# Five rotating lanes for the RG-LRU recurrence: the convolution of tile j+1 issued ahead of the decays of tile j

## The chip, the cores and the metric

One core of one Trainium2 chip runs the whole kernel. The metric is the device time of one execution in microseconds (us). PE is TensorE's matmul side, PEld its weight loads, DVE is VectorE, ACT is ScalarE, POOL is GpSimd, SP is the engine that issues most DMAs.

## The reference

One layer over 1024 tokens of width 1024, in float32. After an RMSNorm, one projection gives two 512-wide inputs of a recurrent branch and the queries, keys and values of a windowed attention. The recurrent branch is what the change touches:

```python
lx = causal_depthwise_conv(lx, w_conv[i], b_conv[i])      # 4 taps along the tokens
r  = sigmoid(blockdiag(lx, w_a) + b_a)
ig = sigmoid(blockdiag(lx, w_i) + b_i)
a  = exp(LRU_C * r * log_sigmoid(lam))
h_t = a_t * h_(t-1) + sqrt(1 - a_t**2) * (ig * lx)_t       # scan over 1024 tokens
y_lru = rmsnorm(h * gelu(lg), g_lru_out)
```

Both branches are normed, concatenated, projected and added to x. Then come a squared-ReLU MLP of width 4096, a gated per-layer embedding and a final RMSNorm.

## The kernel before

Everything lies transposed in SBUF: features on the 128 partitions, the 1024 tokens along the free axis, in two halves of 512. Every product runs as three matmuls (L451 to L453): each float32 operand is split into a high part (ACT copies) and a low part (DVE or POOL subtracts). Weights come in pieces of two halves: SP loads `stage`, ACT writes `w_hi` (`high`, L724), POOL writes `w_lo` (`low`, L353).

The input projection is 28 groups of 24 matmuls; group g goes to bank g % 4 and waits until DVE has emptied that bank from group g-4 (`evac`, L1036, which multiplies by the norm and signals main_free). Groups 0 to 7 give the four tiles (128 channels) of the recurrence's input, 8 to 15 the gelu inputs `gl`, 16 to 19 keys and values, 20 to 27 the queries. Into this stream the recurrence of the four tiles is woven. For tile j, with GATE_AT = [5, 9, 13, 17]:

- DVE: `conv(j)` (L1072) makes `lru_x` from `yl[:, j]` in one tensor_scalar and three scalar_tensor_tensor steps. `lru_x` is a single buffer, so from tile 1 on conv(j) waits for state_done of tile j-1.
- ACT: `gate_input_high(j)` (L790) copies `lru_x` to `gx_hi` in two halves. POOL: `gate_input_low(j)` (L382) writes `gx_lo` in two halves.
- PE: `gates(j)` (L502), 12 matmuls in the middle of group 6, 10, 14 or 18, six for each half, each six waiting for gx_low.
- ACT: `lru_gates(j)` (L796): four sigmoids, a tanh, an exponential. From tile 1 on they wait for state_done of tile j-1.
- DVE: `decays(j)` (L1089), ACT: the root (L823), DVE: `states(j)` (L1102), a multiplication and the scan along the tokens, from `lru_x` into `yl[:, j]`.

The queues are in program order. DVE's order is the loop at L1199:

```python
for g in range(4, IN_GROUPS - 2):
    if g + 1 in GATE_AT[1:]:
        conv(GATE_AT.index(g + 1))
    evac(g)
    if g - 1 in GATE_AT:
        decays(GATE_AT.index(g - 1))
    if g - 2 in GATE_AT:
        states(GATE_AT.index(g - 2))
```

conv(0) stands ahead of the loop (L1135). ACT's order is the loop at L811: at g = 8, 12, 16 it copies two halves of `w_hi`, at g = 5, 9, 13, 17 it makes gx_hi and the gate functions, at the g after that the root, and at 15 and 18 two Gelus. POOL's loop (L391) makes the two halves of `w_lo` and then `gx_lo` of one tile in each turn. Behind the projection follow `multiply_y`, squares and norm of the branch (`norm_y`, `low_y`), and the attention, whose values `v_win` (16 chunks of keys' values, turned on PE and copied by ACT at L840) lie at T + 8 KB, over `lru_u` and `lru_x`.

Of the kernel before, what the change touches and what calls it, by code (L numbers as in the profile page):

```python
# [9 lines left out]
ALU = mybir.AluOpType  # L10
ACT = mybir.ActivationFunctionType
AX = mybir.AxisListType

P = 128
SEQ = 1024
# [4 lines left out]
LT = LRU // P  # L20
# [68 lines left out]
def build(nc, x, p, vectors, gates_w, w_in, w_out, w_ff1, w_ff2, w_ple_gate, w_ple_proj, alibi, out):  # L89
    ctx = ExitStack()  # L90
    with ctx:
# [3 lines left out]
        def at(name, offset, shape, dt=F32):  # L95
            return nc.alloc_sbuf_tensor_at(name, shape, dt, offset=base + offset)
# [23 lines left out]
        lru_r = at("lru_r", T, [P, SEQ])  # L120
        lru_i = at("lru_i", T + 4 * KB, [P, SEQ])
        lru_u = at("lru_u", T + 8 * KB, [P, SEQ])
        lru_x = at("lru_x", T + 12 * KB, [P, SEQ])
        yl = at("yl", Y, [P, LT, SEQ])
        gl = at("gl", G, [P, LT, SEQ])
        r_lru = at("r_lru", G + 12 * KB, [P, SEQ])

        qT = at("qT", Q, [P, SEQ // CHUNK, LT, CHUNK])
        kT = at("kT", KV, [P, PAD + SEQ])
        vT = at("vT", KV + 4 * (PAD + SEQ), [P, PAD + SEQ])  # L130
        v_win = at("v_win", T + 8 * KB, [P, SEQ // CHUNK, P])
        prob = at("prob", G, [P, 2, 1024])
        probT = at("probT", G + 8 * KB, [P, 1024])
        bias = at("bias", G + 12 * KB, [P, 512])
# [71 lines left out]
        def half(hf):  # L206
            return slice(hf * HALF, (hf + 1) * HALF)
# [4 lines left out]

        def q_tile(j, hf):
            return qT[:, hf * 8:(hf + 1) * 8, j, :]

        def by_chunk(ap):
            return ap.rearrange("p (c q) -> p c q", q=CHUNK)
# [127 lines left out]
        def _(pool):  # L345
# [36 lines left out]
            def gate_input_low(j):  # L382

                if j >= 1:
                    pool.wait_ge(gates_done, 4 * j)
                for hf in range(2):
                    pool.wait_ge(gx_high, 2 * j + hf + 1)
                    pool.tensor_tensor(gx_lo[:, half(hf)], lru_x[:, half(hf)], gx_hi[:, half(hf)], ALU.subtract
                                       ).then_inc(gx_low, 1)

            for n in range(2, IN_PIECES):  # L391
# [56 lines left out]
        def _(pe):  # L448
# [110 lines left out]
            def values(u):  # L559

                pe.wait_ge(pt0_read, u + 1)
                pe.wait_ge(pt1_read, u + 1)
                if u >= 1:
                    pe.wait_ge(o_read, u)
                else:
                    pe.wait_ge(main_free, L0)
                for cp in range(2):
                    for g in range(NKV):
                        last = pe.matmul(bank[3][g * HD:(g + 1) * HD, cp * 256:(cp + 1) * 256],  # L569
                                         v_win[:, 2 * u + cp, g * HD:(g + 1) * HD],  # L570
                                         probT[:, g * 512 + cp * 256:g * 512 + (cp + 1) * 256],
                                         start=True, stop=True)
                last.then_inc(o_done, 1)
# [149 lines left out]
        def _(act):  # L723
# [66 lines left out]
            def gate_input_high(j):  # L790

                act.wait_ge(conv_done, j + 1)
                for hf in range(2):
                    act.activation(gx_hi[:, half(hf)], lru_x[:, half(hf)], ACT.Copy).then_inc(gx_high, 1)

            def lru_gates(j):  # L796

# [13 lines left out]
            for g in range(IN_GROUPS):  # L811
                if g % 4 == 0 and g >= 4:
                    n = g // 4 + 1
                    piece_free(act, n - 2)
                    high(2 * n)
                    high(2 * n + 1)
                if g in GATE_AT:
                    gate_input_high(GATE_AT.index(g))
                    lru_gates(GATE_AT.index(g))
                if g - 1 in GATE_AT:  # L820
                    j = GATE_AT.index(g - 1)
                    act.wait_ge(lru_m2, j + 1)
                    act.activation(lru_u[:, :], lru_u[:, :], ACT.Sqrt).then_inc(lru_root, 1)  # L823
                if g in (15, 18):
                    for j in (2 * (g == 18), 2 * (g == 18) + 1):
                        act.wait_ge(main_free, 12 if g == 15 else 16)
                        act.activation(gl[:, j, :], gl[:, j, :], ACT.Gelu_apprx_tanh).then_inc(gelu_done, 1)
                if g in (20, 21):
                    hf = g - 20
                    act.wait_ge(state_done, LT)  # L830
                    for j in range(LT):
                        act.wait_ge(y_done, j + 1)
                        square(SQ_BY[SS_LRU + hf] - 4 + j, sq, yl[:, j, half(hf)])
                if g in (22, 23):
                    root(SS_LRU + g - 22, 5, r_lru, LRU)
                if 21 <= g < 25:
                    i = g - 21
                    act.wait_ge(vt_done, i + 1)
                    act.wait_ge(state_done, LT)
                    act.activation(v_win[:, 4 * i:4 * i + 4, :], bank[6 + i % 2][:, :].rearrange(  # L840
                        "p (c d) -> p c d", d=P), ACT.Copy).then_inc(vt_read, 1)

            def exps(u):
                act.wait_ge(max_done, u + 1)
# [6 lines left out]
            def lru_high(hf):  # L851
                act.wait_ge(main_done, IN_GROUPS - 2 + 2 * hf)
                for j in range(LT):
                    act.wait_ge(y_normed, 4 * hf + j + 1)
                    split_high(H_LRU + 4 * hf + j, yl[:, j, half(hf)], None, j, hf)

            lru_high(0)
            exps(0)
# [152 lines left out]
        def _(dve):  # L1011
# [24 lines left out]
            def evac(g):  # L1036

                n, hf, m = g // 4, (g % 4) // 2, g % 2
                dve.wait_ge(main_done, g + 1)
                if n < 2:  # L1040
                    dst = yl[:, 2 * n + m, half(hf)]
                elif n < 4:
                    dst = gl[:, 2 * (n - 2) + m, half(hf)]
                elif n == 4:
                    dst = (kT, vT)[m][:, PAD + hf * HALF:PAD + (hf + 1) * HALF]
                else:
                    dst = q_tile(2 * (n - 5) + m, hf)
                src, r = main_bank(g)[0][:, :], r_mix[:, half(hf)]
                if n >= 5:
                    src, r = by_chunk(src), by_chunk(r)  # L1050
                dve.tensor_tensor(dst, src, r, ALU.mult).then_inc(main_free, 1)
# [20 lines left out]
            def conv(j):  # L1072

                dve.wait_ge(main_free, 4 if j < 2 else 8)
                if j >= 1:
                    dve.wait_ge(state_done, j)
                link(dve.tensor_scalar(lru_x[:, :], yl[:, j, :], v_conv[:, 12 + j:13 + j], v_bconv[:, j:j + 1],
                                       ALU.mult, ALU.add))
                for s in (1, 2, 3):
                    c = 4 * (3 - s) + j  # L1080
                    ins = dve.scalar_tensor_tensor(out=lru_x[:, s:], in0=yl[:, j, 0:SEQ - s],
                                                   scalar=v_conv[:, c:c + 1], in1=lru_x[:, s:],
                                                   op0=ALU.mult, op1=ALU.add)
                    if s < 3:
                        link(ins)
                    else:
                        ins.then_inc(conv_done, 1)

            def decays(j):  # L1089
# [7 lines left out]

                dve.tensor_scalar(lru_u[:, :], lru_u[:, :], 1e-34, None, ALU.max).then_inc(lru_m2, 1)
                dve.wait_ge(conv_done, j + 1)
                link(dve.tensor_tensor(lru_x[:, :], lru_i[:, :], lru_x[:, :], ALU.mult))  # L1100

            def states(j):  # L1102
                dve.wait_ge(lru_root, j + 1)
                link(dve.tensor_tensor(lru_x[:, :], lru_x[:, :], lru_u[:, :], ALU.mult))
                dve.tensor_tensor_scan(yl[:, j, :], lru_r[:, :], lru_x[:, :], 0.0, ALU.mult, ALU.add
                                       ).then_inc(state_done, 1)


            dve.memset(kT[:, 0:PAD], 0.0).then_inc(pads_ready, 1)
# [28 lines left out]
            def multiply_y(j):  # L1138
                dve.wait_ge(gelu_done, j + 1)
                dve.wait_ge(state_done, j + 1)  # L1140
                dve.tensor_tensor(yl[:, j, :], yl[:, j, :], gl[:, j, :], ALU.mult).then_inc(y_done, 1)

            def norm_y(hf):

                for j in range(LT):
                    dve.wait_ge(sq_done, SQ_BY[SS_LRU + hf] - 3 + j)
                    dve.scalar_tensor_tensor(out=yl[:, j, half(hf)], in0=yl[:, j, half(hf)],
                                             scalar=v_lru[:, j:j + 1], in1=r_lru[:, half(hf)],
                                             op0=ALU.mult, op1=ALU.mult).then_inc(y_normed, 1)

            def low_y(hf):
                for j in range(LT):
                    dve.wait_ge(y_normed, 4 * hf + j + 1)
                    split_low(H_LRU + 4 * hf + j, yl[:, j, half(hf)], None, j, hf)

            def softmax_front(u):

# [39 lines left out]
                dve.tensor_tensor(dst, main_bank(L0 + g)[0][:, :], dst, ALU.add).then_inc(main_free, 1)  # L1197

            for g in range(4, IN_GROUPS - 2):  # L1199
                if g + 1 in GATE_AT[1:]:  # L1200
                    conv(GATE_AT.index(g + 1))
                evac(g)
                if g - 1 in GATE_AT:
                    decays(GATE_AT.index(g - 1))
                if g - 2 in GATE_AT:
# [234 lines left out]
```

## Time and profile before

| what | value |
|---|---|
| runs of the kernel | 1176.6, 1175.78, 1176.55 us; median 1176.55 |
| profiled execution, first to last instruction (span) | 1174.1 us |
| median of the runs less that span | 2.45 us |
| mean granted TensorE clock | 0.985 |

For the profiled execution only the span is known; a run's time also has what lies around the first and last instruction, and it is set beside the median by the 2.45 us in the table. A row of a timeline has the start, the duration, the engine, the line and operation, out<-in, the shape and the count; in brackets stands how long the engine was idle before and what released it. Several like instructions in a row are merged (x2); a row's start is then that of the first.

### The profile page before, as it was taken

How to read it: one execution, taken by the hardware profiler on the slowest of the kernel's cores; microseconds unless marked ns; L12 is line 12 of the kernel's file. 1: busy time of each engine (PE TensorE's matmuls, PEld its weight loads, DVE VectorE, ACT ScalarE, POOL GpSimd, SP SyncE). 2: the span in 40 equal slices, each digit the busy share in tenths (PEclk: the TensorE clock that was granted, in tenths of full speed). 3: DMA queues.
4: the chain of work that ended last, by engine and by line, in shares of the span. 5: the costliest groups of instructions: out<-in, count | busy, mean ns of one | idle time of the engine just before them, and what ended most of it. 6: DMA issues, size and time to landing. Idle time of an engine off the chain costs nothing.

```text
span 1174.1 us, 13976 instructions
## 1 busy us (share of the span) xinstructions
PE 1120.6 (95%) x5196; PEld 922.6 (79%) x5196; DVE 692.3 (59%) x869; ACT 363.6 (31%) x597; POOL 394.9 (34%) x207
## 2 busy tenths in 40 slices
PE   7999899899989999999999999999999999989996
PEld 5777688677768888888888888888888888867995
DVE  6966848767996445445444444444444434586677
ACT  8544554345532211211111111111111111445445
POOL 2633252330481311311311212212213113376874
PEclk9999999899989999999999999999999999989998
DMA  7211102110221111111211201211211211122243
GB/s 269 73 36 36 36 1 81 37 37 1 72 72 36 52 56 36 55 52 36 63 44 36 71 36 36 71 36 36 71 36 41 66 36 53 54 72 72 99 153 109
DMA packets 22481, 69.43 MB, mean 59 GB/s; under 512 B 2352, under 2 KB 4400, under 8 KB 22448
## 3 DMA queue, kind: packets, MB, share of 16 engines
q1 hardware_dynamic: 22176, 67.95, 17.1%
q10 hardware_dynamic: 272, 1.05, 0.2%
q8 instruction: 20, 0.33, 0.1%
q14 instruction: 13, 0.11, 0.0%
HBM read 64.79 MB, written 4.19 MB: 59 GB/s over the span
## 4 chain that ended last, share of the span: by engine, by line
PE 84%; DVE 10%; issue 3%; ACT 1%; DMA 1%; SPq 0%; DVEq 0%
PE bank L451 27%; PE bank L452 27%; PE bank L453 27%; DVE h_lo L1029 4%; DVE xT L1257 1%; DVE r_mix L1034 1%; PE bank L541 1%; DVE scaled L1255 1%; PE bank L569 1%; DMA stage<-in_w_in 1%; PE bank L555 1%; DVE o_ring L1354 1%; PE bank L499 1%; DVE acc L272 0%; DVE xT L1305 0%
## 5 line engine op out<-in xcount | busy, mean ns | idle before, releaser
L451 PE MATMUL bank<-h_hi,w_hi 128*128 128x512 f32 (+1 forms) x1056 | 407.6, 386 | 25.3 <-DVE h_lo L1029 17.5
L452 PE MATMUL bank<-h_lo,w_hi 128*128 128x512 f32 (+1 forms) x1056 | 400.4, 379 | 0.0
L453 PE MATMUL bank<-h_hi,w_lo 128*128 128x512 f32 (+1 forms) x1056 | 400.3, 379 | 0.0
L421 POOL TENSOR_TENSOR w_lo<-stage,w_hi 128x1024 fp32r<-128x1024 f32 x64 | 152.6, 2405 | 524.4 <-ACT w_hi L927 524.4
L1305 DVE TENSOR_TENSOR xT<-bank,xT 128x512 f32<-128x512 f32 x256 | 176.2, 690 | 142.7 <-PE bank L453 142.4
L451 PEld LDWEIGHTS bank<-h_hi,w_hi 128*128 128x128 f32 x1056 | 200.7, 190 | 72.7 <-issue 10.2
L452 PEld LDWEIGHTS bank<-h_lo,w_hi 128*128 128x128 f32 x1056 | 200.8, 190 | 37.3 <-issue 1.7
L453 PEld LDWEIGHTS bank<-h_hi,w_lo 128*128 128x128 f32 x1056 | 200.3, 190 | 37.4
L451 PE MATMUL bank<-u_hi,w_hi 128*128 128x512 f32 x512 | 199.2, 389 | 0.0
L452 PE MATMUL bank<-u_lo,w_hi 128*128 128x512 f32 x512 | 199.2, 389 | 0.0
L453 PE MATMUL bank<-u_hi,w_lo 128*128 128x512 f32 x512 | 199.2, 389 | 0.0
L1290 DVE SCALAR_TENSOR_TENSOR relu<-bank,r_ffn 128x512 f32<-128x512 f32 x64 | 44.2, 691 | 213.4 <-PE bank L453 212.9
L927 ACT ACTIVATE w_hi<-stage 128x1024 fp32r<-128x1024 f32 x64 | 64.0, 1048 | 286.9 <-DVE xT L1305 286.9
L359 POOL TENSOR_TENSOR w_lo<-stage,w_hi 128x1024 fp32r<-128x1024 f32 x45 | 120.7, 2702 | 86.9 <-ACT w_hi L730 86.9
L938 ACT ACTIVATE u_hi<-relu 128x512 fp32r<-128x512 f32 x64 | 40.5, 633 | 279.4 <-DVE relu L1290 279.4
L451 PEld LDWEIGHTS bank<-u_hi,w_hi 128*128 128x128 f32 x512 | 96.1, 188 | 19.9
L452 PEld LDWEIGHTS bank<-u_lo,w_hi 128*128 128x128 f32 x512 | 96.1, 188 | 19.9
L453 PEld LDWEIGHTS bank<-u_hi,w_lo 128*128 128x128 f32 x512 | 96.1, 188 | 19.9
L272 POOL TENSOR_TENSOR acc<-acc,sq 128x512 f32<-128x512 f32 (+1 forms) x60 | 77.8, 1297 | 53.3 <-ACT sq L752 39.0
L1029 DVE SCALAR_TENSOR_TENSOR h_lo<-xT,vec,h_hi 128x512 fp32r<-128x512 f32 x48 | 62.6, 1325 | 3.7 <-ACT h_hi L744 3.5
L1294 DVE TENSOR_TENSOR usq<-relu 128x512 f32<-128x512 f32 x64 | 50.1, 783 | 2.2
L730 ACT ACTIVATE w_hi<-stage 128x1024 fp32r<-128x1024 f32 x45 | 44.9, 1046 | 6.1 <-PE bank L453 6.1
(141 smaller groups left out, 845.6 us busy)
## 6 DMA issues: line engine op xcount, KB each, us to landing
stage<-in_w_ff SPq DMA_DIRECT2D x64, 512.0 KB, 3.3
stage<-in_w_ple_gate SPq DMA_DIRECT2D x24, 512.0 KB, 3.3
stage<-in_w_in SPq DMA_DIRECT2D x13, 512.0 KB, 3.3
stage<-in_w_out SPq DMA_DIRECT2D x8, 512.0 KB, 3.5
xT<-in_x SPq DMA_DIRECT2D x7, 512.0 KB, 9.4
out_x<-o_ring SPq DMA_DIRECT2D x4, 512.0 KB, 4.0
out_x<-o_ring SPq DMA_DIRECT2D x7, 256.0 KB, 2.2
pT<-in_p ACTq DMA_DIRECT2D x1, 1024.0 KB, 7.7
```

The costliest lines, as they stand in the source:

```text
L272: eng.tensor_tensor(dst, dst, src, ALU.add).then_inc(sq_used, 1)
L359: pool.tensor_tensor(lo, stage[:, s % STAGES, :], hi, ALU.subtract).then_inc(w_split, 1)
L421: pool.tensor_tensor(w_lo[:, n0 % 2, o:o + HP], stage[:, s0 % STAGES, :], w_hi[:, n0 % 2, o:o + HP], ALU.subtract).then_inc(w_split, 1)
L451: pe.matmul(o, whi, hh, start=first, stop=False)
L452: pe.matmul(o, whi, hl, start=False, stop=False)
L453: return pe.matmul(o, wlo, hh, start=False, stop=last)
L730: act.activation(hi, stage[:, s % STAGES, :], ACT.Copy).then_inc(w_high, 1)
L927: act.activation(w_hi[:, n0 % 2, o:o + HP], stage[:, s0 % STAGES, :], ACT.Copy).then_inc(w_high, 1)
L1029: dve.scalar_tensor_tensor(out=o, in0=src, scalar=scale, in1=hi, op0=ALU.mult, op1=ALU.subtract).then_inc(h_ready, 1)
L1290: dve.scalar_tensor_tensor(out=relu[:, j % 2, :], in0=bank[j][:, :], scalar=0.0, in1=r_ffn[:, half(hf)], op0=ALU.max, op1=ALU.mult).then_i ...
L1294: dve.tensor_tensor(usq[:, j % 2, :], relu[:, j % 2, :], relu[:, j % 2, :], ALU.mult).then_inc(u_sq, 1)
L1305: dve.tensor_tensor(dst, bank[4 + q % 4][:, :], dst, ALU.add).then_inc(y_added, 1)
```

## The change

The single buffer `lru_x` and the four tiles of `yl` become one tile `lane` of five buffers. The projection's tile j is evacuated into lane j+1 (`lx(j)`). The convolution of tile j reads lane j+1 and writes lane j (`yl(j)`), which is free as soon as conv(j-1) has read it; the gate product, the multiplication by the root and the scan then work in place in lane j. conv(j+1) waits for conv_done of tile j instead of its state_done, and stands behind the evacuation of groups 4, 8 and 12, that is ahead of decays(j). Two waits are added: ACT waits for gates_done of tile j-1 before it overwrites `gx_hi` (POOL had that wait already), and DVE waits for gx_low before it multiplies lane j in place. As lane 0 now lies where the second half of `v_win` was, `v_win` becomes two tiles, `v_first` in its old place and `v_second` over lane 4.

```diff
-        lru_x = at("lru_x", T + 12 * KB, [P, SEQ])
-        yl = at("yl", Y, [P, LT, SEQ])
+        lane = at("lane", T + 12 * KB, [P, LT + 1, SEQ])
...
-        v_win = at("v_win", T + 8 * KB, [P, SEQ // CHUNK, P])
+        v_first = at("v_first", T + 8 * KB, [P, SEQ // CHUNK // 2, P])
+        v_second = at("v_second", Y + 12 * KB, [P, SEQ // CHUNK // 2, P])
...
+        def lx(j):
+            return lane[:, j + 1, :]
+
+        def yl(j):
+            return lane[:, j, :]
+
+        def v_win(c):
+            return (v_first, v_second)[c // 8], c % 8
...
-                    pool.tensor_tensor(gx_lo[:, half(hf)], lru_x[:, half(hf)], gx_hi[:, half(hf)], ALU.subtract
+                    pool.tensor_tensor(gx_lo[:, half(hf)], yl(j)[:, half(hf)], gx_hi[:, half(hf)], ALU.subtract
...
                 act.wait_ge(conv_done, j + 1)
+                if j >= 1:
+                    act.wait_ge(gates_done, 4 * j)
                 for hf in range(2):
-                    act.activation(gx_hi[:, half(hf)], lru_x[:, half(hf)], ACT.Copy).then_inc(gx_high, 1)
+                    act.activation(gx_hi[:, half(hf)], yl(j)[:, half(hf)], ACT.Copy).then_inc(gx_high, 1)
...
                 if n < 2:
-                    dst = yl[:, 2 * n + m, half(hf)]
+                    dst = lx(2 * n + m)[:, half(hf)]
...
                 if j >= 1:
-                    dve.wait_ge(state_done, j)
-                link(dve.tensor_scalar(lru_x[:, :], yl[:, j, :], v_conv[:, 12 + j:13 + j], v_bconv[:, j:j + 1],
-                                       ALU.mult, ALU.add))
+                    dve.wait_ge(conv_done, j)
+                o, x_j = yl(j), lx(j)
+                link(dve.tensor_scalar(o, x_j, v_conv[:, 12 + j:13 + j], v_bconv[:, j:j + 1], ALU.mult, ALU.add))
                 for s in (1, 2, 3):
                     c = 4 * (3 - s) + j
-                    ins = dve.scalar_tensor_tensor(out=lru_x[:, s:], in0=yl[:, j, 0:SEQ - s],
-                                                   scalar=v_conv[:, c:c + 1], in1=lru_x[:, s:],
-                                                   op0=ALU.mult, op1=ALU.add)
+                    ins = dve.scalar_tensor_tensor(out=o[:, s:], in0=x_j[:, 0:SEQ - s], scalar=v_conv[:, c:c + 1],
+                                                   in1=o[:, s:], op0=ALU.mult, op1=ALU.add)
...
                 dve.wait_ge(conv_done, j + 1)
-                link(dve.tensor_tensor(lru_x[:, :], lru_i[:, :], lru_x[:, :], ALU.mult))
+                dve.wait_ge(gx_low, 2 * j + 2)
+                link(dve.tensor_tensor(yl(j), lru_i[:, :], yl(j), ALU.mult))
...
-                link(dve.tensor_tensor(lru_x[:, :], lru_x[:, :], lru_u[:, :], ALU.mult))
-                dve.tensor_tensor_scan(yl[:, j, :], lru_r[:, :], lru_x[:, :], 0.0, ALU.mult, ALU.add
-                                       ).then_inc(state_done, 1)
+                link(dve.tensor_tensor(yl(j), yl(j), lru_u[:, :], ALU.mult))
+                dve.tensor_tensor_scan(yl(j), lru_r[:, :], yl(j), 0.0, ALU.mult, ALU.add).then_inc(state_done, 1)
...
             for g in range(4, IN_GROUPS - 2):
-                if g + 1 in GATE_AT[1:]:
-                    conv(GATE_AT.index(g + 1))
                 evac(g)
+                if g + 1 in GATE_AT:
+                    j = GATE_AT.index(g + 1) + 1
+                    if j < LT:
+                        conv(j)
                 if g - 1 in GATE_AT:
                     decays(GATE_AT.index(g - 1))
```

The other places that read `yl[:, j]` or `v_win` (squares, norm, splits, the value matmuls and their copies) read the same data under the new names.

## Rows read from the trace of the kernel before

**Rows 1.** The page's first part: busy us of each engine, share of the span, instructions.
```profile
PE 1120.6 (95%) x5196; PEld 922.6 (79%) x5196; DVE 692.3 (59%) x869; ACT 363.6 (31%) x597; POOL 394.9 (34%) x207
```

**Rows 2.** Waits of PE, 50 to 165 us: us in total, times, longest.
```profile
PE bank L451 <- issue: 11.2, 4, 4.2
```

**Rows 3.** Timeline of PE: start us, us, operation [idle before, releaser].
```profile
51.88 0.47 PE L451 MATMUL bank<-gx_hi,gw_hi 128*128 128x512 f32 x1 [1.25 <-issue]
...
76.25 0.39 PE L453 MATMUL bank<-h_hi,w_lo 128*128 128x512 f32 x1
79.56 0.61 PE L451 MATMUL bank<-gx_hi,gw_hi 128*128 128x512 f32 x1 [2.92 <-issue]
...
105.53 0.39 PE L453 MATMUL bank<-h_hi,w_lo 128*128 128x512 f32 x1
108.80 0.47 PE L451 MATMUL bank<-gx_hi,gw_hi 128*128 128x512 f32 x1 [2.89 <-issue]
...
111.65 0.39 PE L451 MATMUL bank<-h_hi,w_hi 128*128 128x512 f32 x1
...
137.76 0.77 PE L451 MATMUL bank<-gx_hi,gw_hi 128*128 128x512 f32 x1 [4.19 <-issue]
...
142.18 0.39 PE L451 MATMUL bank<-h_hi,w_hi 128*128 128x512 f32 x1
```

**Rows 4.** Windows: length, busy us by engine (PE, PEld, DVE, ACT, POOL), PEclk, DMA.
```profile
77.00:86.00 9.00, 6.44 (x21) 5.22 (x22) 1.58 (x3) 5.94 (x8) 2.50 (x2) 0.81 0.00 0
...
106.00:134.00 28.00, 24.77 (x108) 20.20 (x108) 18.89 (x15) 15.98 (x17) 7.70 (x4) 1.00 0.09 30
134.00:143.00 9.00, 5.24 (x16) 4.26 (x17) 6.93 (x6) 4.68 (x7) 3.48 (x2) 0.81 0.06 25
...
165.00:200.00 35.00, 35.00 (x174) 28.06 (x173) 19.80 (x26) 14.32 (x33) 14.93 (x8) 1.00 0.19 68
```

**Rows 5.** Timeline of ACT: root, w_hi copies, gx_hi, and the exponential of tile 2.
```profile
63.32 1.06 ACT L823 ACTIVATE lru_u<-lru_u 128x1024 f32<-128x1024 f32 x1 [2.71 <-DVE lru_u L1098]
64.29 1.99 ACT L730 ACTIVATE w_hi<-stage 128x1024 fp32r<-128x1024 f32 x2
77.42 1.15 ACT L794 ACTIVATE gx_hi<-lru_x 128x512 fp32r<-128x512 f32 x2 [11.13 <-DVE lru_x L1081]
...
116.10 1.15 ACT L809 ACTIVATE lru_r<-lru_r,lam 128x1024 f32<-128x1024 f32 x1
...
121.26 1.06 ACT L823 ACTIVATE lru_u<-lru_u 128x1024 f32<-128x1024 f32 x1 [2.71 <-DVE lru_u L1098]
```

**Rows 6.** Timeline of POOL: the pairs of w_lo and of gx_lo.
```profile
65.41 7.46 POOL L359 TENSOR_TENSOR w_lo<-stage,w_hi 128x1024 fp32r<-128x1024 f32 x2 [12.39 <-ACT w_hi L730]
78.19 2.50 POOL L388 TENSOR_TENSOR gx_lo<-lru_x,gx_hi 128x512 fp32r<-128x512 f32 x2 [5.31 <-ACT gx_hi L794]
...
126.67 5.20 POOL L359 TENSOR_TENSOR w_lo<-stage,w_hi 128x1024 fp32r<-128x1024 f32 x2 [16.73 <-ACT w_hi L730]
```

**Rows 7.** Timeline of DVE: evacuations, decays, scans, first convolution step.
```profile
54.74 1.28 DVE L1051 TENSOR_TENSOR yl<-bank,r_mix 128x512 f32<-128x512 f32 x2
...
59.35 1.23 DVE L1092 SCALAR_TENSOR_TENSOR lru_u<-lru_r,lru_u 128x1024 f32<-128x1024 f32 x1 [1.02 <-ACT lru_r L809]
...
66.31 4.37 DVE L1105 TENSOR_TENSOR_SCAN yl<-lru_r,lru_x 128x1024 f32<-128x1024 f32 x1
70.79 2.63 DVE L1077 TENSOR_SCALAR lru_x<-yl,vec 128x1024 f32<-128x1024 f32 x1
...
117.28 1.23 DVE L1092 SCALAR_TENSOR_TENSOR lru_u<-lru_r,lru_u 128x1024 f32<-128x1024 f32 x1 [2.02 <-ACT lru_r L809]
...
124.25 2.29 DVE L1105 TENSOR_TENSOR_SCAN yl<-lru_r,lru_x 128x1024 f32<-128x1024 f32 x1
```

**Rows 8.** Line 1081, the convolution's later steps: count, duration ns min/median/max.
```profile
L1081 DVE SCALAR_TENSOR_TENSOR lru_x<-yl,vec,lru_x x12: 1281/1284/3297, 43.8 to 134.3; 128x1023 f32<-128x1023 f32 x4, 128x1022 f32<-128x1022 f32 x4, 128x1021 f32<-128x1021 f32 x4
```

**Rows 9.** Timeline of PE, 205 to 335 us: the only wait of that stretch.
```profile
214.79 1.97 PE L569 MATMUL bank<-probT,v_win 128*64 128x256 f32 x8 [5.16 <-issue]
```

More of the change, by code:

```diff
@@ L567, in values @@
                 for cp in range(2):
+                    v, c = v_win(2 * u + cp)
                     for g in range(NKV):
                         last = pe.matmul(bank[3][g * HD:(g + 1) * HD, cp * 256:(cp + 1) * 256],
-                                         v_win[:, 2 * u + cp, g * HD:(g + 1) * HD],
+                                         v[:, c, g * HD:(g + 1) * HD],
                                          probT[:, g * 512 + cp * 256:g * 512 + (cp + 1) * 256],
@@ L832, in _ @@
                         act.wait_ge(y_done, j + 1)
-                        square(SQ_BY[SS_LRU + hf] - 4 + j, sq, yl[:, j, half(hf)])
+                        square(SQ_BY[SS_LRU + hf] - 4 + j, sq, yl(j)[:, half(hf)])
                 if g in (22, 23):
@@ L839, in _ @@
                     act.wait_ge(state_done, LT)
-                    act.activation(v_win[:, 4 * i:4 * i + 4, :], bank[6 + i % 2][:, :].rearrange(
-                        "p (c d) -> p c d", d=P), ACT.Copy).then_inc(vt_read, 1)
+                    v, c = v_win(4 * i)
+                    act.activation(v[:, c:c + 4, :], bank[6 + i % 2][:, :].rearrange("p (c d) -> p c d", d=P), ACT.Copy
+                                   ).then_inc(vt_read, 1)
             def exps(u):
@@ L854, in lru_high @@
                     act.wait_ge(y_normed, 4 * hf + j + 1)
-                    split_high(H_LRU + 4 * hf + j, yl[:, j, half(hf)], None, j, hf)
+                    split_high(H_LRU + 4 * hf + j, yl(j)[:, half(hf)], None, j, hf)
             lru_high(0)
@@ L1140, in multiply_y @@
                 dve.wait_ge(state_done, j + 1)
-                dve.tensor_tensor(yl[:, j, :], yl[:, j, :], gl[:, j, :], ALU.mult).then_inc(y_done, 1)
+                dve.tensor_tensor(yl(j), yl(j), gl[:, j, :], ALU.mult).then_inc(y_done, 1)
             def norm_y(hf):
@@ L1146, in norm_y @@
                     dve.wait_ge(sq_done, SQ_BY[SS_LRU + hf] - 3 + j)
-                    dve.scalar_tensor_tensor(out=yl[:, j, half(hf)], in0=yl[:, j, half(hf)],
+                    dve.scalar_tensor_tensor(out=yl(j)[:, half(hf)], in0=yl(j)[:, half(hf)],
                                              scalar=v_lru[:, j:j + 1], in1=r_lru[:, half(hf)],
@@ L1153, in low_y @@
                     dve.wait_ge(y_normed, 4 * hf + j + 1)
-                    split_low(H_LRU + 4 * hf + j, yl[:, j, half(hf)], None, j, hf)
+                    split_low(H_LRU + 4 * hf + j, yl(j)[:, half(hf)], None, j, hf)
             def softmax_front(u):
```

## The prediction

> **What bounds the kernel now.** I began with the page's busy shares: TensorE (PE) is busy for 1120.6 us, 95% of the span [rows 1], so a change in the recurrence pays only where it removes time in which PE waits or runs slowly. The list of PE's waits, cut to the stretch from 50 to 165 us, holds four waits and nothing else, 11.2 us together [rows 2]. The timeline of PE shows where they are: each ends in the first gate matmul of a tile (51.88, 79.56, 108.80, 137.76), with 1.25, 2.92, 2.89 and 4.19 us idle before it [rows 3]. The profile calls the releaser "issue", so the code has to name it: a gate matmul waits for gx_low, which POOL sends after ACT's gx_hi, which waits for the convolution, which waits for the scan of the tile before. The rows of ACT and POOL agree: gx_hi starts at 77.42 after an 11.13 us wait for the convolution, and gx_lo at 78.19 [rows 5, 6].
>
> Two waits cost more than their length. In the stretches 77 to 86 and 134 to 143 us the granted clock is 0.81, against 1.00 in a warm stretch: part of each ran at 1.2 GHz instead of 2.4, behind the waits of 2.92 and 4.19 us [rows 4]. The twelve gate matmuls take 142.18 - 137.76 = 4.42 us there and 111.65 - 108.80 = 2.85 us when warm: 1.57 us lost. For tile 1, 79.56 to 105.92 (105.53 + 0.39) is 26.36 us, against 76.64 - 51.88 = 24.76 us for the same work when warm: 1.60 us lost [rows 3].
>
> So the three waits between tiles cost 2.92 + 2.89 + 4.19 + 1.57 + 1.60 = 13.2 us. That is all that the change can reach here; the wait of 1.25 us before tile 0 stays, as that convolution is not moved.
>
> **The change part by part.** *The dependence removed.* conv(j+1) no longer waits for state_done of tile j; it needs only its own lane and conv_done of tile j, and is issued four groups earlier. The 13.2 us go if the rest of the way to gx_lo is shorter than the 24.76 us of PE work per tile. It is not short, because two queues still put gx behind tile j: ACT issues gx_hi(j+1) after the root of tile j and two w_hi copies, and POOL issues gx_lo(j+1) after the two w_lo that follow from them. I walk this way, counting from the first gate matmul of tile j.
> - ACT's exponential ends at 116.10 + 1.15 = 117.25, which is 8.45 us after 108.80; the decays start at 8.48 (117.28) and the root at 12.46 (121.26) [rows 3, 5, 7].
> - From the root to the w_hi copies is 64.29 - 63.32 = 0.97 us and from there to POOL's first w_lo 65.41 - 64.29 = 1.12 us: POOL starts at 14.55 [rows 5, 6].
> - POOL's pair takes 7.46 us beside a multiplication and the scan and 5.20 us beside one convolution step [rows 6]. With the scan it ends at 22.0.
> - Here the moved convolution of the tile after next falls. VectorE (DVE) and POOL take turns: the convolution's first step lasts 2.63 us and ends at 73.42, 0.55 us after POOL's pair ended at 72.87; the scan lasts 4.37 us beside POOL and 2.29 alone; the later steps last 1.28 us alone and up to 3.30 beside POOL [rows 6 to 8]. I take alternation: 0.55 us of DVE, the first half of gx_lo in 2.50/2= 1.25 us [rows 6], ending at 23.8, then 1.28 us of DVE and the second half, ending at 26.3.
>
> PE asks for the first half at 24.76 and, six matmuls of 0.23 us later, for the second at 26.1. The loop closes with about a microsecond to spare on the first half and 0.2 us short on the second.
>
> *The rule behind the turns.* The Trainium skill (SBUF — State Buffer, section "Who interferes with whom") says that the two engines share a port pair, that whoever starts first keeps it for its whole instruction and that the other blocks. It speaks against this change, which puts four two-input or scalar steps of DVE where POOL prepares gx_lo; the rows above agree with it. By it the sum is the one below; without any blocking it would be the full 13.2 us, 1163.4 us.
>
> *Tile by tile.* Tile 0 to 1: conv(1) now stands between two evacuations, where POOL is idle: 0.55 + 3 x 1.28 and small gaps, 4.6 us. It starts at 54.74 + 0.60, two more evacuations of 0.60 follow, and the decays of tile 0 start at 54.74 + 0.6 + 4.6 + 1.2 = 61.1 instead of 59.35 [rows 7], 1.8 us late. All that follows moves with it: root 65.1, w_lo 67.2, pair done 74.6, first half 76.45, second 79.0. PE asks at 76.64 and 78.0: a wait of **1.0 us** is left. Tile 1 to 2: PE is itself 1.0 us later, and asks for the halves at 25.8 and 27.1 against 23.8 and 26.3: **0**. Tile 2 to 3: two Gelu passes stand between root and copies (121.26 to POOL's 126.67, 5.41 us instead of 2.09), but no convolution is left beside POOL, so the pair takes 4.65 us (5.20 less one step of 0.55) and ends at 22.5; first half at 23.8, second near 26.3 after a multiplication of 1.2 us takes its turn: **0.2 us**. Bounds for the left-over sum: 0 (POOL gets two turns running) and 6 us (each half loses one more DVE step of 1.28 us, at all tiles, with one fall of the clock).
>
> *Clock.* Gaps of 1.25 and 2.89 us were not followed by a slow stretch [rows 3, 4], so the gaps left should not cost more. Bounds: none or one more of 1.6 us anywhere.
>
> *Work moved and waits added.* The same convolution, decays and scans are issued, so DVE's total stays. Evacuations of groups 5 and 6 stand behind conv(1), 4 us later, but PE needs those banks only four groups on; likewise groups 9, 10, 13 and 14. ACT's new wait for gates_done and DVE's new wait for gx_low name events 10 us old: nothing. No DMA and nothing on SP moves.
>
> *In-place scan.* No row shows one. In-place multiplications exist throughout, at ordinary speed. Bounds: 2.29 us alone, 4.37 as seen beside POOL; I take 2.29. The scan of tile 0 ends 1.8 us later than before even if blocked again, at 66.31 + 4.37 + 1.8 = 72.5; ACT needs its state_done only for the next sigmoid, after the gates at 77 have begun, so some 5 us hide either. *v_win in two tiles* is the same four copies: nothing.
>
> *What is late next.* After tile 3's gates no queue's order changes. Evacuations, norms and scores start from PE's groups, so the rest should move as a block, with the 5.16 us wait at 214.79 [rows 9] in it. Bound: 0 to all of the gain given back.
>
> **Sum**: -13.2 + 1.0 + 0 + 0.2 = -12.0 us. The profiled span is 1174.1 us and becomes 1162.1; the median of the runs, 2.45 us above that span, goes from 1176.55 to 1164.55, say **1164.6 us**.
>
> **Rivals.** *A. The queue replaces the dependence*: POOL loses more turns, and gx_lo is about 2 us late at each tile; with one slow stretch 3 x 2.0 + 1.6 = 7.6 us stay where I left 1.2: 1171 us. For it: the margin above is one microsecond in 25, and the order in which the two engines take turns can change with a small shift. Against: in every row above they alternate. *B. No blocking at the moved place*: POOL's two instructions follow each other before DVE; 1163.4 us. *C. Nothing net*: the attention stretch, where DVE is nearly full, waits longer and takes the gain; about 1176 us. Against: PE does not wait from 137.76 to 209.6 (busy without a break from 165 to 200 [rows 4]), and what DVE does there starts from PE's groups. This is also where it would lie if the change did not do what it says, since gx still stands behind the root in ACT's queue. *D. Slower*: a scan that reads and writes the same lane runs several times slower. ACT's sigmoid waits for state_done; the scan has 5 us to spare, so it decides from 7.5 us upward. To eat the 12 us and another 2.4 at three tiles takes 4.8 us more, a scan of 12 us: 1179 us. Against: the scan's other input was already read beside a write to another lane at 2.29 us, and in-place operations show no penalty.
>
> **How the numbers follow.** Forecast 0.62 (1163.6 to 1166.5), A 0.18 (1166.5 to 1172), B 0.12 (1161.5 to 1163.6), C 0.05, D 0.03. The range keeps the first case, B whole with a clock stretch in its favour, and A's first half: 1161.5 to 1169.5. 0.2% of the time is 2.35 us, about what a measurement of this kernel can tell from no change; only C and D are within it or slower: faster 0.93, same 0.04, slower 0.03.
>
> **What would show it.** Right: conv(1) near 55 to 60 us with no wait of ACT for it; the decays of tile 0 near 61; gates of tile 1 near 77 with about 1 us of waiting in their second half; gates of tiles 2 and 3 near 102 and 127 with next to none; a clock of 1.00 from 50 to 165; all later rows 12 us earlier. Wrong: waits of 2 us or more before gates 2 or 3 (A); a scan over 4.4 us (D); a wait longer than 5.2 us before the first values, or new ones behind it (C).

## The result and the profile after

| kernel | runs | median us | ratio to the kernel before, 95% interval |
|---|---|---|---|
| before, beside the first runs | 4 | 1176.16 | |
| changed, first runs | 4 | 1166.03 (1163.47 to 1166.95) | 0.9901 (0.9883 to 0.9918) |
| before, beside the second runs | 20 | 1177.80 | |
| changed, second runs | 5 | 1165.68 | 0.9892 (0.9873 to 0.9910) |
| before, beside the third runs | 9 | 1177.52 | |
| changed, third runs | 5 | 1166.28 | 0.9903 (0.9886 to 0.9919) |

The change saves about 1%: 11 to 13 us by the three ratios, while the medians beside each other lie 10.1, 12.1 and 11.2 us apart. The forecast was 1164.6, 1.4 us under the first median, with a range of 1161.5 to 1169.5. The profiled execution took 1165.31 us, with a span of 1163.5 against 1174.1 before. Two runs at a much lower granted clock are left out of all figures here, one of the kernel before (1880.38 us at 0.558) and one of the kernel with more work in POOL's queue (1263.03 us at 0.847).

The page's first line and the list of PE's waits from 50 to 155 us answer to [rows 1, 2]. The second row is a wait inside tile 1's gates.

```profile
PE 1120.2 (96%) x5196; PEld 922.9 (79%) x5196; DVE 690.1 (59%) x869; ACT 363.8 (31%) x597; POOL 397.4 (34%) x207
...
PE bank L460 <- issue: 1.3, 1, 1.3
PE bank L460 <- POOL gx_lo L397: 0.5, 1, 0.5
```

PE is as busy as before in microseconds; of the 11.2 us of waits, 1.8 are left. The timeline of PE answers to [rows 3]: the first gate matmul of each tile, and the two places inside the gates where it still stops.

```profile
50.74 0.47 PE L460 MATMUL bank<-gx_hi,gw_hi 128*128 128x512 f32 x1 [1.28 <-issue]
...
75.42 0.47 PE L460 MATMUL bank<-gx_hi,gw_hi 128*128 128x512 f32 x1
...
77.59 0.50 PE L460 MATMUL bank<-gx_hi,gw_hi 128*128 128x512 f32 x1 [0.55 <-POOL gx_lo L397]
...
100.84 0.39 PE L460 MATMUL bank<-gx_hi,gw_hi 128*128 128x512 f32 x1
...
125.32 0.39 PE L460 MATMUL bank<-gx_hi,gw_hi 128*128 128x512 f32 x1
...
126.46 0.39 PE L462 MATMUL bank<-gx_hi,gw_lo 128*128 128x512 f32 x1
126.91 0.50 PE L460 MATMUL bank<-gx_hi,gw_hi 128*128 128x512 f32 x1
```

The gates of tiles 2 and 3 follow the matmul before them without a gap, at 100.84 and 125.32; a wait of 0.22 us shows inside tile 3's (126.91 instead of 126.69). The windows that answer to [rows 4] show a clock of 1.00 where it was 0.81 behind the waits:

```profile
77.00:86.00 9.00, 8.45 (x38) 6.98 (x38) 6.22 (x7) 8.02 (x9) 0.54 (x1) 1.00 0.00 0
...
126.00:135.00 9.00, 8.93 (x40) 7.08 (x39) 3.89 (x4) 8.58 (x9) 0.86 (x1) 1.00 0.00 1
```

The next rows follow the way to gx_lo, one fence for each engine's timeline, ACT, POOL and DVE, as in [rows 5 to 7].

```profile
64.05 1.06 ACT L835 ACTIVATE lru_u<-lru_u 128x1024 f32<-128x1024 f32 x1 [4.57 <-DVE lru_u L1110]
65.02 2.00 ACT L740 ACTIVATE w_hi<-stage 128x1024 fp32r<-128x1024 f32 x2
66.92 1.14 ACT L806 ACTIVATE gx_hi<-lane 128x512 fp32r<-128x512 f32 x2
```

```profile
66.14 7.48 POOL L368 TENSOR_TENSOR w_lo<-stage,w_hi 128x1024 fp32r<-128x1024 f32 x2 [14.26 <-ACT w_hi L740]
73.58 3.96 POOL L397 TENSOR_TENSOR gx_lo<-lane,gx_hi 128x512 fp32r<-128x512 f32 x2
...
118.61 4.77 POOL L368 TENSOR_TENSOR w_lo<-stage,w_hi 128x1024 fp32r<-128x1024 f32 x2 [17.24 <-ACT w_hi L740]
```

```profile
54.21 0.80 DVE L1091 TENSOR_SCALAR lane<-lane,vec 128x1024 f32<-128x1024 f32 x1
55.05 3.92 DVE L1094 SCALAR_TENSOR_TENSOR lane<-lane,vec 128x1023 f32<-128x1023 f32 x3
...
60.09 1.22 DVE L1104 SCALAR_TENSOR_TENSOR lru_u<-lru_r,lru_u 128x1024 f32<-128x1024 f32 x1
...
67.05 4.38 DVE L1118 TENSOR_TENSOR_SCAN lane<-lru_r,lane 128x1024 f32<-128x1024 f32 x1
...
71.93 2.24 DVE L1091 TENSOR_SCALAR lane<-lane,vec 128x1024 f32<-128x1024 f32 x1
74.20 5.73 DVE L1094 SCALAR_TENSOR_TENSOR lane<-lane,vec 128x1023 f32<-128x1023 f32 x3
...
116.20 2.29 DVE L1118 TENSOR_TENSOR_SCAN lane<-lru_r,lane 128x1024 f32<-128x1024 f32 x1
```

ACT no longer waits for a convolution before gx_hi: it copies at 66.92, right behind the weight copies. What PE waits for is now the next link, POOL, which starts gx_lo the moment its pair of weights is done (73.58, no idle time before it). The convolution takes 4.8 us where POOL is idle (54.21 to 58.97) and 8.0 where it is not (71.93 to 79.93).

**Where the time went.** I cut both profiled executions at the first gate matmul of tile 0 and at the first values matmul [rows 3, 9], the latter of the changed kernel being:

```profile
201.03 1.98 PE L579 MATMUL bank<-probT,v_first 128*64 128x256 f32 x8 [5.18 <-issue]
```

The middle piece went from 162.91 to 150.29 us: 12.6 us gained. The piece ahead of it was 1.1 us shorter (50.74 against 51.88); in the next profile of the same kernel it was 51.85, so that is the run's. The piece behind it was 3.2 us longer (962.5 against 959.3). The three make the 10.6 us of the span. The 3.2 us lie in the last stage, the gated embedding: windows of the kernel before, then of the changed one, at the same work.

```profile
1060.00:1070.00 10.00, 8.09 (x36) 6.38 (x35) 9.11 (x10) 3.88 (x6) 5.83 (x3) 1.00 0.15 52
...
1140.00:1150.00 10.00, 10.00 (x84) 9.94 (x83) 9.86 (x13) 5.94 (x12) 7.98 (x6) 1.00 0.55 196
```

```profile
1047.00:1057.00 10.00, 6.84 (x24) 5.42 (x24) 8.38 (x9) 3.69 (x5) 5.84 (x3) 0.83 0.15 52
...
1127.00:1137.00 10.00, 9.45 (x65) 9.40 (x65) 9.89 (x14) 5.20 (x11) 7.48 (x5) 0.83 0.64 211
```

At these two places the granted clock fell in this execution and not in the one of before, where it had been down for longer some 20 us ahead of the first (shown at the end of this document). Whether the change does that is one question for the runs below.

### The profile page after: what moved, and what is told of

Same layout as the page of the kernel before. It is cut to its first block, busy times and chain, and to the rows that moved or that the text cites. A ratio compares the mean times of both kernels' runs of the same rounds, so it can differ in the third digit from the quotient of the medians.

```text
span 1163.5 us, 13983 instructions
## 1 busy us (share of the span) xinstructions
PE 1120.2 (96%) x5196; PEld 922.9 (79%) x5196; DVE 690.1 (59%) x869; ACT 363.8 (31%) x597; POOL 397.4 (34%) x207
## 3 DMA queue, kind: packets, MB, share of 16 engines
HBM read 64.79 MB, written 4.19 MB: 59 GB/s over the span
## 4 chain that ended last, share of the span: by engine, by line
PE 83%; DVE 12%; issue 2%; POOL 1%; ACT 1%; DMA 1%; SPq 0%; DVEq 0%; ACTq 0%
PE bank L460 27%; PE bank L461 26%; PE bank L462 26%; DVE h_lo L1042 4%; DVE r_mix L1047 1%; DVE xT L1271 1%; PE bank L550 1%; DVE lane L1094 1%; DVE scaled L1269 1%; PE bank L579 1%; POOL gx_lo L397 1%; PE bank L508 1%; PE bank L564 1%; DMA stage<-in_w_in 1%; POOL w_lo L368 1%
## 5 line engine op out<-in xcount | busy, mean ns | idle before, releaser
L940 ACT ACTIVATE w_hi<-stage 128x1024 fp32r<-128x1024 f32 x64 | 64.1, 1049 | 286.8 <-DVE xT L1319 286.8
L762 ACT ACTIVATE sq<-xT 128x512 f32<-128x512 f32 (+1 forms) x72 | 41.5, 577 | 17.5 <-POOL acc L279 7.6
```

The lines of the kernel that those rows point to most:

```text
L762: act.activation(dst, src, ACT.Square).then_inc(sq_done, 1)
L940: act.activation(w_hi[:, n0 % 2, o:o + HP], stage[:, s0 % STAGES, :], ACT.Copy).then_inc(w_high, 1)
```

## The experiments

The theory: the gain is the removed dependence, and what is left hangs on POOL's queue. Rivals: the layout or the in-place scan has an effect of its own; the freed loop has room to spare, and the 0.55 us is an accident; the change lengthens the end.

**The changed kernel again**, no edit.

> The changed kernel once more, for a second profile and a narrower interval. Theory: the waits of PE between 50 and 155 us are the same as in the first profile (1.3 us before the first gates, about 0.5 us inside tile 1's, at most 0.2 us inside tile 3's), and from the first gate matmul of tile 0 to the first values matmul it takes 150.3 us again (162.9 in the kernel before). What differs between runs lies behind, in the last 130 us, where the granted clock falls to half in some of them: 1.6 us for each fall, 1163 to 1167 us in all. Rival, that the lanes themselves vary (turns taken between VectorE and GpSimd): the stretch of the recurrence differs by 1 us or more between the two profiles.

Measured: 1165.68 us. 1.3 us before the first gates and 0.55 inside tile 1's; the middle piece is 202.14 - 51.85 = 150.29 us, the same to the hundredth, and the end 962.6. The stretch of the recurrence repeats; the end's length was the long one again.

**The kernel before again**, no edit.

> The kernel before once more, for a second profile of it. Theory: waits of 1.25, 2.9, 2.9 and 4.2 us before the gates, two of them followed by a slow stretch of 1.6 us or, if the clock's falls are a matter of the run, one or three; 162.9 us from the first gate matmul to the first values matmul, within 1.7 us. Rival, that the first profile was an odd one: waits that differ by over 0.5 us.

Measured: 1180.13 us (one run). PE's first gate matmuls of tiles 1 to 3:

```profile
78.95 0.77 PE L451 MATMUL bank<-gx_hi,gw_hi 128*128 128x512 f32 x1 [2.92 <-issue]
...
108.32 0.47 PE L451 MATMUL bank<-gx_hi,gw_hi 128*128 128x512 f32 x1 [3.15 <-issue]
...
137.83 0.77 PE L451 MATMUL bank<-gx_hi,gw_hi 128*128 128x512 f32 x1 [3.17 <-issue]
```

The first wait agrees, the third is a microsecond shorter than in the first profile, which the expectation missed; by the bound of 0.5 us that it set, the rival holds there. The clock fell behind all three this time (0.81, 0.86 and 0.65 in the windows behind them), so the middle piece was 164.66 us. And its end was 962.4 us: the long end occurs without the change.

**The old order in the new layout.** Five lanes, in-place scan and split v_win stay; the convolution goes back behind the scan of the tile before.

```diff
+                if g + 1 in GATE_AT[1:]:
+                    conv(GATE_AT.index(g + 1))
                 evac(g)
-                if g + 1 in GATE_AT:
-                    j = GATE_AT.index(g + 1) + 1
-                    if j < LT:
-                        conv(j)
```

> All of the change but its order: five lanes, in-place scan and v_win in two tiles as in the changed kernel, while the convolution of tile j+1 is issued at its old place behind the scan of tile j. Theory (the gain is the removed dependence alone, the lanes only allow it): waits of 2.9, 2.9 and 4.2 us before the gates of tiles 1 to 3 return, 1175 to 1177 us, ratio to the kernel before 0.999 to 1.001. Rival (the layout or the in-place scan has an effect of its own): more than 2 us away from that, on either side; an in-place scan that is slower would show as over 2.29 us where GpSimd is idle.

Measured: 1176.42 us over 10 runs, ratio 0.9984 (0.9968 to 1.0001), a little under the 0.999 to 1.001 expected, which the interval holds too. PE's gate matmuls with a wait:

```profile
79.46 0.77 PE L460 MATMUL bank<-gx_hi,gw_hi 128*128 128x512 f32 x1 [2.91 <-issue]
...
108.82 0.47 PE L460 MATMUL bank<-gx_hi,gw_hi 128*128 128x512 f32 x1 [3.19 <-issue]
...
137.99 0.47 PE L460 MATMUL bank<-gx_hi,gw_hi 128*128 128x512 f32 x1 [2.79 <-issue]
140.16 0.50 PE L460 MATMUL bank<-gx_hi,gw_hi 128*128 128x512 f32 x1 [0.54 <-POOL gx_lo L397]
```

The waits are back and the gain is gone: the middle piece is 162.48 us. The scan takes 2.29 us in place where POOL is idle. The last wait came out shorter than the 4.2 expected because PE came later, not gx_lo earlier: the gates of tile 3 begin at 137.99 us, where the first profile of before has 137.76, but the clock had fallen behind the gates of tile 2. The same stretch in that profile, then here:

```profile
106.00:118.00 12.00, 9.20 (x41) 7.62 (x42) 3.24 (x5) 9.18 (x11) 2.50 (x2) 1.00 0.00 0
...
106.00:118.00 12.00, 9.18 (x33) 7.44 (x34) 2.67 (x5) 8.69 (x11) 2.52 (x2) 0.86 0.00 0
```

The second profile of before has 0.86 there, too, and a third wait of 3.17 us ending at 137.83. In this kernel the convolution no longer waits for state_done, only its place in DVE's queue holds it behind the scan, so taking the wait out is of no use unless the convolution is moved as well. So the order makes the gain, and the layout only allows it; a gain from the layout of more than 0.32% lies outside the interval, and so does any loss over 0.01%.

**More work in POOL's queue.** POOL computes one half of the low weights twice ahead of gx_lo of tiles 1 to 3; `again(s)`, whose definition is left out here, waits for the same half of `w_hi` as `low(s)` and does the same subtraction.

```diff
                 low(2 * n)
+                if 1 <= n - 2 < LT:
+                    again(2 * n + 1)
                 low(2 * n + 1)
                 if n - 2 < LT:
                     gate_input_low(n - 2)
```

> The changed kernel, with GpSimd writing one half of the low weights twice (about 2.4 us of queue more) ahead of gx_lo of tiles 1, 2 and 3. Theory (the way through the root, the weight copies and GpSimd's queue has become the limit, with about 0, 1.5 and 0.7 us to spare at tiles 1, 2, 3): the waits at the three gates grow to about 2.5 to 3.5, 1 to 2 and 1.7 to 2.5 us, 5 to 8 us in all, 1.6 us more if the clock falls behind one: 1170 to 1176 us. Rival (the freed loop has room, the 0.5 us left is an accident): waits under 1 us each, within 1.5 us of the changed kernel.

Measured: 1174.31 us over nine runs, ratio 0.9965 (0.9951 to 0.9978). PE's waits:

```profile
79.98 0.47 PE L469 MATMUL bank<-gx_hi,gw_hi 128*128 128x512 f32 x1 [3.21 <-issue]
...
107.78 0.47 PE L469 MATMUL bank<-gx_hi,gw_hi 128*128 128x512 f32 x1 [1.35 <-issue]
...
109.96 0.51 PE L469 MATMUL bank<-gx_hi,gw_hi 128*128 128x512 f32 x1 [0.55 <-POOL gx_lo L404]
...
135.18 0.47 PE L469 MATMUL bank<-gx_hi,gw_hi 128*128 128x512 f32 x1 [1.80 <-issue]
...
137.35 0.50 PE L469 MATMUL bank<-gx_hi,gw_hi 128*128 128x512 f32 x1 [0.55 <-POOL gx_lo L404]
```

3.21, 1.90 and 2.35 us at the three tiles, each inside the range that the margins of 0, 1.5 and 0.7 us gave. With one fall of the clock behind the first (0.83 from 77 to 87 us) the middle piece is 159.43 us, so one more POOL instruction per tile takes back 9.1 of the 12.6 us. The extra instruction takes 2.39 us where DVE is idle (tile 3) and 4.38 us beside DVE's scan (tiles 1 and 2). The rival of a loop with room to spare falls.

**gx_lo ahead of the low weights in POOL's queue.**

```diff
-                low(2 * n)
-                low(2 * n + 1)
-                if n - 2 < LT:
+                if 1 <= n - 2 < LT:
                     gate_input_low(n - 2)
+                low(2 * n)
+                low(2 * n + 1)
+                if n == 2:
+                    gate_input_low(0)
```

> The changed kernel, with GpSimd writing gx_lo of tiles 1 to 3 ahead of the pair of low weights instead of behind it; ScalarE's order is untouched. Theory (GpSimd's queue, not the convolution, holds what is left): no wait of PE at the gates of tiles 1 to 3, the first gate matmul of tile 0 to the first values matmul 149.5 us instead of 150.3, the time 0.8 us less; the low weights come 4 us later, which their groups do not notice. Rival (ScalarE's order, the root ahead of gx_hi, holds it): the 0.55 us inside tile 1's gates stay.

Measured: 1163.08 us, ratio 0.9879 (0.9858 to 0.9899). POOL's rows, and the only wait of PE from 40 to 150 us:

```profile
68.08 4.46 POOL L397 TENSOR_TENSOR gx_lo<-lane,gx_hi 128x512 fp32r<-128x512 f32 x2 [15.79 <-ACT gx_hi L808]
72.50 6.72 POOL L368 TENSOR_TENSOR w_lo<-stage,w_hi 128x1024 fp32r<-128x1024 f32 x2
...
PE bank L462 <- issue: 1.3, 1, 1.3
```

No wait is left at tiles 1 to 3, with ACT's order as it was. The middle piece is 200.00 - 51.15 = 148.85 us, 1.44 less than in the changed kernel, of which 0.77 are the waits of 0.55 and 0.22. The rest is around them. The 0.55 counts from the end of a matmul of 0.40 us; by the starts, its successor comes 0.95 us after it instead of 0.23 (76.64 and 77.59), a loss of 0.72. The first gate matmul of tile 1 was 0.08 us late as well (75.42, 0.31 after the one before). With the 0.22 that makes 1.02 us, and the three matmuls from each of these three stops on take 0.77 to 0.80 us instead of 0.68, 0.33 more.

**ACT's gx_hi ahead of the root as well.**

```diff
                 if g in GATE_AT:
-                    gate_input_high(GATE_AT.index(g))
-                    lru_gates(GATE_AT.index(g))
+                    j = GATE_AT.index(g)
+                    if j == 0:
+                        gate_input_high(0)
+                    lru_gates(j)
+                    if j + 1 < LT:
+                        gate_input_high(j + 1)
```

> As the run before it, and ScalarE copies gx_hi of tile j+1 right behind the gate functions of tile j, ahead of the root and the weight copies. Theory: gx of the next tile is then ready some 10 us early, no wait at the gates of tiles 1 to 3, 149.5 us for the stretch and no further gain over GpSimd's order alone, since PE had nothing left to wait for; within 0.5 us of that run. Rival (GpSimd's gx_lo now takes turns with the decays and delays the scan): the stretch is over 150.3 us, with waits at the gates or at the left recurrence's norm.

Measured: 1163.16 us, ratio 0.9868 (0.9851 to 0.9884); the middle piece is 148.88 us. The same as POOL's order alone, to 0.03 us: PE had nothing left to wait for. DVE's decays do take turns with gx_lo now (the first two of tile 0 take 2.07 and 1.67 us instead of 1.22 and 0.69), and no wait of PE follows from it.

**And the first gates later**: the gates of tile 0 behind group 6 instead of in its middle.

```diff
-                if g - 1 in GATE_AT:
+                if g - 1 in GATE_AT[1:]:
                     middle = lambda: gates(GATE_AT.index(g - 1))
...
                 group(g, n, KD, m, hf, 0, None, g % 4 == 0, middle)
+                if g - 1 == GATE_AT[0]:
+                    gates(0)
```

> As gx ahead of the root, and the gates of tile 0 are issued at the end of group 6 instead of in its middle, 2.7 us of matmuls later. Theory: the wait of 1.3 us before the first gates goes as well, no wait of PE is left between 40 us and the first values matmul, which comes 2.1 us earlier than in the changed kernel counted from the start of group 4 (165.5 us there, 163.4 here); about 1163.5 us, the best of all. Rival (what depends on tile 0's gates, its decays and the root, moves the 2.7 us into later waits): a wait of over 0.5 us at the gates of tile 1 or at the low weights of group 12.

Measured: 1163.23 us, ratio 0.9874 (0.9858 to 0.9891). PE has no wait from 40 to 150 us, so the rival's wait did not come; the first values matmul stands at

```profile
198.98 1.98 PE L581 MATMUL bank<-probT,v_first 128*64 128x256 f32 x8 [5.17 <-issue]
```

162.52 us after the start of group 4 (36.46), against 165.50 in the changed kernel: 3.0 us less, where 2.1 were forecast. But the median is that of the two kernels before it, and the profiled end is 962.1 us. The time thus showed nothing of these 3 us, so three kernels were run once more side by side.

> The changed kernel beside the two below on one chip. Theory: from the first gate matmul of tile 0 to the first values matmul 150.3 us for the third time; from there to the end either about 959.2 or about 962.4 us, the two lengths that all profiles so far fall into, with and without the change; times from 1163 to 1167 us. Rival (the change makes the end longer): 962.4 in every profile of kernels with the early convolution.

> GpSimd's gx_lo ahead of its low weights, once more, for the comparison on one chip. Theory: 148.9 us for the stretch again, 1.4 us under the changed kernel in the time (ratio to it 0.9988), half of which was forecast from the waits and the rest is the restart of PE behind each. Rival: the difference of 2.6 us between the medians of the two earlier calls is the chip's, and on one chip they are within 0.5 us.

> gx ahead of the root and the first gates later, once more. Theory: 162.5 us from the start of group 4 to the first values matmul, 3.0 us under the changed kernel, and both lengths of the end occur, so that its lowest time lies 1.5 us under the lowest of the kernel with GpSimd's order alone. Rival (the end takes back what is gained ahead of it): no run under 1162 us, as in the first four.

Measured side by side, beside 1177.52 us of the kernel before: the changed kernel 1166.28, POOL's order 1164.39 (0.9893, 0.9878 to 0.9908), all three edits **1161.83 us** (0.9865, 0.9847 to 0.9882; lowest run 1159.82). The pieces repeat: 150.26 us in the changed kernel, 162.55 from group 4 with all three edits; with POOL's order alone 149.28, as the wait before the values was 5.55 us this time. The version with all edits beats both the kernel before and the changed one, by 15.7 and 4.5 us of the medians here; 3.0 of the 4.5 lie in the piece that repeats, the rest goes with the end. The intervals of POOL's order and of the changed kernel overlap, so those two are told apart by the piece and not by the time.

The end was long (962.1 to 962.8 us) in all three profiles of the changed kernel, and with the early convolution also with more work in POOL's queue, with gx ahead of the root and in both profiles with all edits; it was short (959.4 and 959.5) in both with POOL's order alone. Without the early convolution it was short twice (959.3, and 959.1 with the old order in the new layout) and long once. So the early convolution does not force the long end, and the order of before does not exclude it. But whether it makes the long end more frequent, seven of nine profiles against one of three, is not settled: that part of the rival stands, and it would take back up to 3 us of the 12.6.

## Why the prediction was right

*What bounds the kernel.* The three waits and their two slow stretches were 13.2 us by the rows of before; 12.6 us of the middle piece went. The old order alone brings the waits back, so the cause named from the code behind "issue" was the right one. The 13.2 was a little small: with no wait left at the gates (POOL's order changed) the middle piece is 162.91 - 148.85 = 14.1 us shorter. What was left was a little small, too, 1.44 us where 1.2 was summed; the two misses partly cancel, 14.1 - 1.4 against 13.2 - 1.2. Nor are the terms quite independent: a slow stretch behind one tile's gates brings PE later to the next ones and shortens the wait there, as the old order showed.

*The walk to gx_lo.* It named the next limit. Tile 0 to 1: the decays start 9.35 us after the first gate matmul, where 61.1 - 51.88 = 9.2 was worked out; the wait left was 0.55 us instead of 1.0, as POOL's two halves took 3.96 us, less than the 0.55 of DVE, two halves of 1.25 and one step of 1.28 that I summed (4.33). Tile 1 to 2: none, as said. Tile 2 to 3: 0.22 us for 0.2. That the margin is small at every tile was shown by doubling one POOL instruction: a wait came at each.

*The turns.* The scan took 4.38 us beside POOL and 2.29 alone, the convolution's first step 2.24 and 0.80, POOL's pair of weights 7.48 beside the scan and 4.77 alone. The Trainium skill (SBUF — State Buffer, section "Who interferes with whom") says that of two instructions that need the port pair shared by DVE and GpSimd, the one that issues second blocks until the first is done. The scan of tile 0 agrees: it starts at 67.05, 2.22 us before the first of POOL's pair ends (69.27), and takes 2.09 us more than alone. Rival B, no blocking and so no wait, did not occur: 1.4 us of the gain stayed behind.

*Rivals.* A, the queue in place of the dependence, is what happens with one more POOL instruction (3.21, 1.90 and 2.35 us), not in the changed kernel. D fell: in place the scan costs what it did. C did not occur where I put it: the wait before the values stayed at 5.18 us for 5.16.

*The term that was off.* I let all later work move as a block. It did, to within about a microsecond, as far as the last stage, where the profiled execution lost 3.2 us, with two falls of the clock; the sign "all later rows 12 us earlier" fails there. The sum of -12.0 holds for the middle (-12.6), and as a ratio (0.990) it lies within all three intervals; the medians are 1.1 to 1.7 us over the forecast.

## What to carry to other kernels

When a wait is removed, follow the freed operand through every queue it still stands in, and set that length against the work that must cover it: here the way through root, weight copies and POOL left between nothing and 1.7 us in 25. Putting the operand ahead of work with slack in POOL's queue took another 1.4 us off that stretch, the same in ACT's queue nothing more, and the first gates later the rest of 3.0. Cut two profiles at the same instruction before comparing their ends: pieces that repeat within 0.05 us can stand beside pieces that move by 3 us from run to run.

## What the runs showed that was not expected

- A stop of PE costs more than the wait that the list shows: 1.44 us went when waits of 0.77 us were removed, at a clock of 1.00 all along. I had not counted that in the 1.2 us left over.
- Waits before the gates were followed by a slow stretch eight times in four profiles (2.91, 2.92 twice, 3.15, 3.17, 3.19, 3.21 and 4.19 us) and were not at 2.89, 2.79, 1.80 and 1.35. In the last stage a wait of 2.27 us was followed by one in the second profile of the changed kernel and not in the third, so the length of the wait alone does not decide.
- The last stage ends in two lengths about 3 us apart. In the long one PE waits longer for the same DVE result, here in the kernel before and in the changed one, and the clock falls behind it:

```profile
1063.31 0.50 PE L451 MATMUL bank<-h_hi,w_hi 128*128 128x512 f32 x1 [1.91 <-DVE gt L1338]
```

```profile
1050.28 0.79 PE L460 MATMUL bank<-h_hi,w_hi 128*128 128x512 f32 x1 [3.16 <-DVE gt L1352]
```

The kernel before shows 3.23 us at this place in its second profile. Just ahead of it the two lengths differ already, the kernel before first, then the changed one:

```profile
1042.00:1052.00 10.00, 8.90 (x25) 6.46 (x26) 5.80 (x4) 5.50 (x10) 3.44 (x4) 0.66 0.19 67
...
1029.00:1039.00 10.00, 8.75 (x30) 6.53 (x31) 5.95 (x4) 5.50 (x10) 3.58 (x4) 0.83 0.20 73
```

All twelve profiles divide in this way. In the four with the short end the clock there is 0.66 and the wait 1.86 to 1.93 us, with no fall behind it; in the eight with the long end it is 0.83 and the wait 2.93 to 3.23 us, with a fall. So a PE that was slowed less comes early to a DVE result that has not moved with it, and can lose the clock there. What decides how long the clock is down ahead of it was not tried.
